# PSUM operands, another order of products and moved loads, with 512 moving columns in the gate and up projections

## What is computed

```python
# first network, per layer
y = hybrid_mixer(x, ...)            # chunked relative attention, latent attention, forgetting attention,
                                    # each with a gated projection, summed, times w_out
x = layer_norm(alpha * x + y, ...)
x = layer_norm(alpha * x + memory_cross_attention(x, mem, ...), ...)
x = layer_norm(alpha * x + swiglu_ffn(x, ...), ...)
# swiglu_ffn: gu = x @ w_gu; (silu(gu[..., :2816]) * gu[..., 2816:]) @ w_down

# second network, per layer: modulate(rmsnorm(x)), then a mixer of spatial gating (gelu, layernorm over a chunk),
# differential attention with a norm per head, and a short convolution; x += gate * (m @ wo); then
def conv_ffn(h, w_up, cw, cb, w_down):
    u = dwconv3(h @ w_up, cw) + cb           # three taps along the tokens
    g, val = jnp.split(u, 2, axis=-1)
    return (jax.nn.silu(g) * val) @ w_down
```

## Time and profile before

| what | value |
|---|---|
| median of three runs | 2719.44 us (2719.43 to 2723.04) |
| time of the profiled execution | 2722.86 us |
| its span | 2721.1 us |
| granted clock of TensorE, mean | 0.997 |
| TensorE matmul busy | 2677.6 us (98%), 21551 |
| VectorE busy | 1063.0 us (39%) |
| ScalarE busy | 1411.5 us (52%) |
| Gpsimd busy | 1953.0 us (72%) |
| DMA | 182 GB/s |

### The profile page before, as it was taken

One profiled execution on the slowest core, in us unless ns is written; L12 is line 12 of the kernel. 1 busy time (PEld: TensorE's weight loads), 2 busy tenths in 40 slices (PEclk: granted clock), 3 DMA queues, 4 the chain that ended last, 5 costly groups with the idle time before them and its releaser, 6 DMA issues.

```text
span 2721.1 us, 51137 instructions
## 1 busy us (share of the span) xinstructions
PE 2677.6 (98%) x21551; PEld 2505.1 (92%) x21551; DVE 1063.0 (39%) x2123; ACT 1411.5 (52%) x1936; POOL 1953.0 (72%) x816
## 2 busy tenths in 40 slices
PE   8999999999999999999999999999999999999999
PEld 8899989989899899989999998788999988989999
DVE  2433331134334422434434343545443345543434
ACT  5655554447565544455654446456544455565443
POOL 6657668856567488687687887766778877558787
PEclk9999999999999999999999999999999999999999
DMA  7555465565455655564454555544445565445453
GB/s 279 207 193 202 161 243 186 181 224 194 183 218 196 224 183 183 200 205 158 149 169 156 185 187 190 184 147 132 149 159 187 181 214 168 132 132 171 158 184 132
DMA packets 137093, 495.74 MB, mean 182 GB/s; under 512 B 15136, under 2 KB 17440, under 8 KB 135968
## 3 DMA queue, kind: packets, MB, share of 16 engines
q1 hardware_dynamic: 132480, 480.55, 52.4%
q10 hardware_dynamic: 4384, 11.93, 1.2%
HBM read 489.27 MB, written 3.15 MB: 181 GB/s over the span
## 4 chain that ended last, share of the span: by engine, by line
PE 94%; DVE 3%; ACT 2%; DVEq 1%; issue 0%; ACTq 0%; DMA 0%; SPq 0%
PE lin L578 19%; PE lin L582 18%; PE lin L579 18%; PE aux L578 5%; PE aux L579 5%; PE aux L582 5%; PE lin L618 4%; PE lin L619 4%; PE lin L622 4%; PE aux L1103 2%; PE aux L1121 1%; PE aux L799 1%; PE aux L767 1%; PE lin L767 1%; PE aux L1110 1%; DVE Z L1698 1%
## 5 line engine op out<-in xcount | busy, mean ns | idle before, releaser
L547 POOL TENSOR_TENSOR wlo<-raw,whi 128x1024 fp32r<-128x1024 f32 x812 | 1952.8, 2425 | 759.1 <-ACT whi L1210 758.5
L1210 ACT ACTIVATE whi<-raw 128x1024 fp32r<-128x1024 f32 x812 | 845.9, 1057 | 741.4 <-PE lin L582 518.6
L578 PE MATMUL lin<-in_hi,whi 128*128 128x256 f32 x3520 | 880.9, 287 | 20.4 <-ACT whi L1210 8.7
L579 PE MATMUL lin<-in_lo,whi 128*128 128x256 f32 x3520 | 867.2, 283 | 0.0
L578 PEld LDWEIGHTS lin<-in_hi,whi 128*128 128x128 f32 x3520 | 676.1, 192 | 55.9 <-issue 35.1
L579 PEld LDWEIGHTS lin<-in_lo,whi 128*128 128x128 f32 x3520 | 676.9, 192 | 0.5
L582 PE MATMUL lin<-in_hi,wlo 128*128 128x256 f32 x3520 | 501.8, 283 | 0.0
L582 PEld LDWEIGHTS lin<-in_hi,wlo 128*128 128x128 f32 x3520 | 458.4, 193 | 0.0
L578 PE MATMUL aux<-br_hi,whi 128*128 128x256 f32 x880 | 219.1, 283 | 0.0
L579 PE MATMUL aux<-br_lo,whi 128*128 128x256 f32 x880 | 218.9, 283 | 0.0
L578 PE MATMUL lin<-br_hi,whi 128*128 128x256 f32 x768 | 195.5, 288 | 0.0
(11 more groups left out here) (264 smaller groups left out, 3333.4 us busy)
## 6 DMA issues: line engine op xcount, KB each, us to landing
raw<-in_wstream SPq DMA_DIRECT2D x908, 512.0 KB, 3.4
Z<-in_rel ACTq DMA_DIRECT2D x2, 1536.0 KB, 9.5
Z<-in_mem_t ACTq DMA_DIRECT2D x2, 1024.0 KB, 5.3
kv_store<-Z ACTq DMA_DIRECT2D x2, 1024.0 KB, 8.6
Z<-kv_store ACTq DMA_DIRECT2D x2, 1024.0 KB, 11.4
x<-in_x_t SPq DMA_DIRECT2D x2, 512.0 KB, 6.0
Z<-in_ctx_t SPq DMA_DIRECT2D x1, 1024.0 KB, 5.0
out_x<-x SPq DMA_DIRECT2D x4, 256.0 KB, 2.2
```

Of the source, the lines that this page charges most:

```text
L547: pool.tensor_tensor(wlo[s][:, :], raw[i % RAWS][:, :], whi[s][:, :].bitcast(F32), ALU.subtract).then_inc(lo_pool, 1)
L578: pe.matmul(out, wh, xh, start=start, stop=False, skip_group_check=True)
L579: pe.matmul(out, wh, xl, start=False, stop=False, skip_group_check=True)
L1210: act.activation(whi[s % SLOTS][:, :], raw[i % RAWS][:, :], ACT.Copy).then_inc(hi_ready, 1)
```

## The change

In words:

- The high and low inputs become two halves of one tensor `in_both`. In the feed-forward blocks, hidden tiles 2 to 21 are made one at a time by `gate_up`: the high weight by high and low input as one matmul of 512 columns, into a whole PSUM bank, 256 columns of sums for each input; then the low weight by the high input, 256 columns, into the first half. VectorE adds the two halves with a `tensor_reduce` into SBUF. The convolution reads that sum and writes PSUM; the SiLU's input, the product and the rounding's input are in PSUM.
- A tile is two units. The order of units is: the first chunk, tile 2, then tile c and one down unit (three tiles behind) in turn. A half of `lin` is free only when the tile's low part is made.
- Where all eight input tiles are fresh, the first tile's products go in the order high weight by high input, low weight by high input, high weight by low input. The first two wait for `first_hi` alone, the last for `inputs_ready`.
- The merged halves, the GELU of v, and the root of the head norm (`head_root`, 16 columns of `aux`) stay in PSUM; the halves of `lin` are freed later for it.
- A preload of the Exp table is put behind the latent roots. The RMS norm of the last layer comes ahead of the DMA issues at the top of `second_layer`. The wait for the context's inverse goes behind the first hidden tiles.

The core of the diff:

```diff
 def ffn_units(chunk, unit, gu, down):
+    def gate_up(c):
+        at = c // 2 * CH + c % 2 * P
+        for k0 in (0, KD // 2):
+            unit(gu, [(k, at + up) for k in range(k0, k0 + KD // 2) for up in (0, 2 * P)], P)
+    chunk(gu, 0)
+    for c in range(2, HIDDEN):
+        gate_up(c)
+        if FIRST_DOWN <= c <= LAST_DOWN:
+            down_rows(c - FIRST_DOWN)
+    for c in range(LAST_DOWN - FIRST_DOWN + 1, HIDDEN - 2):
+        down_rows(c)
...
-        in_hi, in_lo = sb("in_hi", KD * T, F32R), sb("in_lo", KD * T, F32R)
+        in_both = ctx.enter_context(nc.sbuf_tensor("in_both", [P, 2, KD * T], F32R))
+        in_hi, in_lo = in_both[:, 0, :], in_both[:, 1, :]
...
@@ feature_units (token_units alike) @@
+                        if len(fresh) == KD and ks == (0,):
+                            pe.wait_ge(first_hi, t.next(first_hi))
+                            for j, (c, w) in enumerate(tiles):
+                                pe.matmul(lin[0:w, p, j * T:(j + 1) * T], wh[:, c:c + w], tile(xh, base), start=(j % 2 == 0), stop=False,
+                                          skip_group_check=True)
+                            low_part(low)
+                            for j, (c, w) in enumerate(tiles):
+                                low_product(lin[0:w, p, j * T:(j + 1) * T], wl[:, c:c + w], tile(xh, base), False)
+                            pe.wait_ge(inputs_ready, t.next(inputs_ready))
+                            for j, (c, w) in enumerate(tiles):
+                                low_product(lin[0:w, p, j * T:(j + 1) * T], wh[:, c:c + w], tile(xl, base), False)
+                            continue
...
@@ TensorE @@
+            def gate_up(p, after=()):
+                pe.wait_ge(lin_free[p], t.next(lin_free[p]))
+                for k0 in (0, KD // 2):
+                    wh, wl, low = next_unit()
+                    ...
+                    for k, up, w in blocks:
+                        pe.matmul(lin[:, p, up * CH:(up + 1) * CH], wh[:, w], in_both[:, :, k * T:(k + 1) * T],
+                                  start=(k == 0), stop=(k == KD - 1), skip_group_check=True)
+                    low_part(low)
+                    for k, up, w in blocks:
+                        mm = low_product(lin[:, p, up * CH:up * CH + T], wl[:, w], tile(in_hi, k), k == KD - 1)
...
@@ ScalarE, first_fill @@
+                act.preload_act_table(ACT.Exp)
...
@@ ScalarE, ffn @@
+                def hidden(c, units, behind=0):
+                    hi_parts(units)
+                    ...
+                    act.activation(silu_tile(conv, c), gate, ACT.Silu).then_inc(glu_ready, 1)
+                    hi_parts(behind)
+                    act.wait_ge(hid_f32, t.next(hid_f32))
+                    act.activation(hidden_tile(br_hi, c), gated_tile(p), ACT.Copy).then_inc(hid_hi, 1)
+                for c in range(2, HIDDEN - 1):
+                    hidden(c, 3 if c > FIRST_DOWN else 2)
...
@@ VectorE, ffn @@
+                def hidden(c, count):
+                    p = (c + 1) % 2
+                    both, h = gate_and_up(p), gated_tile(p)
+                    chunk_done(count)
+                    u = summed(conv, c)
+                    i = dve.tensor_reduce(three(u, 2), both.rearrange("p a (s t) -> p a t s", s=2), AX.X, ALU.add)
+                    if conv:
+                        settle()
+                        convolved([u[:, i * T:(i + 1) * T] for i in range(2)], [both[:, i, 0:T] for i in range(2)], taps(c))
+                        settle().then_inc(conv_out, 1)
+                        value = both[:, 1, 0:T]
+                    else:
+                        ...
+                    dve.wait_ge(glu_ready, t.next(glu_ready))
+                    tt_(h, silu_tile(conv, c), value, ALU.mult).then_inc(hid_f32, 1)
+                    settle()
+                    dve.wait_ge(hid_hi, t.next(hid_hi))
+                    tt_(hidden_tile(br_lo, c), h, hidden_tile(br_hi, c).bitcast(F32), ALU.subtract).then_inc(hid_lo, 1)
+                    settle().then_inc(lin_free[p], 1)
...
@@ VectorE, first_layer @@
-                    out = merged[:, half(d)]
+                    out = lin[:, 1 - d, :]
                     chunk_done(2)
-                    tt_(out, zt(GATES + 16 + 4 * d, 4), lin[:, 1 - d, :], ALU.mult).then_inc(lin_free[1 - d], 1)
+                    tt_(out, zt(GATES + 16 + 4 * d, 4), out, ALU.mult)
                     settle()
                     tt_(out, out, two[:, half(d)], ALU.add)
...
-                evacuate(1, 4, zt(GB + 4, 4), func=ACT.Gelu_apprx_tanh)
+                hi_parts(4)
+                units_done()
+                act.activation(lin[:, 1, :], lin[:, 1, :], ACT.Gelu_apprx_tanh)
...
-                    vt = zt(GB + 4 + 2 * tt, 2)
-                    last = dve.tensor_scalar(vt, vt, small[:, 40 + 2 * tt:41 + 2 * tt], small[:, 14 + tt:15 + tt],
+                    last = dve.tensor_scalar(zt(GB + 4 + 2 * tt, 2), lin[:, 1, tt * CH:(tt + 1) * CH], small[:, 40 + 2 * tt:41 + 2 * tt], small[:, 14 + tt:15 + tt],
                                              ALU.subtract, ALU.mult)
...
-                ss, var, ok, r = small[:, 208:224], small[:, 160:176], small[:, 192:208], small[:, 176:192]
+                ss, var, ok, r = small[:, 208:224], small[:, 160:176], small[:, 192:208], head_root
```

More of the change, by code:

```diff
@@ L630, in token_units @@
                     for i, ks in enumerate(runs):
+                        if len(fresh) == KD and ks == (0,):
+                            pe.wait_ge(first_hi, t.next(first_hi))
+                            halves = [(lin[:, p, tt * CH:(tt + 1) * CH], slice(tt * P, (tt + 1) * P)) for tt in range(2)]
+                            for out, s in halves:
+                                pe.matmul(out, xh[:, s], wh[:, 0:CH], start=True, stop=False, skip_group_check=True)
+                            low_part(low)
+                            for out, s in halves:
+                                token_low(out, xh[:, s], wl[:, 0:CH], False)
+                            pe.wait_ge(inputs_ready, t.next(inputs_ready))
+                            for out, s in halves:
+                                token_low(out, xl[:, s], wh[:, 0:CH], False)
+                            continue
                         for k in ks:
@@ L1467, in ffn, with first_tiles @@
             def ffn(conv, context_norm=False):
-                def hidden(j, units, behind=0):
-                    p, b = j % 2, j % 3
+                def first_tiles(units):
                     hi_parts(units)
@@ new lines, in ffn @@
+                first_tiles()
+                if context_norm:
+                    dve.wait_ge(inverse_wide, t.next(inverse_wide))
+                    copy(ctx_scale, inverse_out(0)).then_inc(ctx_inverse, 1)
+                    settle()
+                for c in range(2, HIDDEN):
+                    hidden(c, 3 if FIRST_DOWN < c < HIDDEN - 1 else 2)
+                    if context_norm and c % 4 == 1 and c < HIDDEN - 2:
+                        context_quarter(c // 4 - 1)
+                lo_parts(3)
```

213 lines of the change are left out of this document (107 added, 106 removed).

## The result

The changed kernel takes **2684.32 us** (median of 4 runs, 2683.75 to 2685.24), beside 2720.69 us (2719.43 to 2723.04) for the kernel before in the same comparison: ratio 0.9866, 95% interval 0.9849 to 0.9883. The prediction was 2681.7 us with a range from 2672 to 2704. The profiled execution took 2683.82 us; its span is 39.2 us shorter than that of the earlier trace rows, where the sum of the prediction had 37.7.

The account below looks back on a forecast made before the run. TensorE's matmuls were taken to bound the kernel; 21.3 - 2.0 + 8.4 + 2.8 + 2.0 + 3.3 + 1.9 + 0 = 37.7 us, against the median of 2719.44, gave 2681.7 us, range 2672 to 2704.

Parts of the forecast that it names:

- Bound by TensorE: Whole kernel: it ends when TensorE has got through its matmuls, which make up 94% of the chain that ended last.
- 512 columns, 21.3: Gate and up of five feed-forward blocks: 1600 pairs merged into 512-column matmuls, 13.3 ns less each, 21.3 us saved.
- a pair costs 0.2400 now and 0.2267 after: Gate and up: cost in us of two 256-column products against one of 512, taken from the nearest 512-column row.
- rival (1): Gate and up: a 512-column product over two runs costs what two of 256 do; gain 16.4, time 2703.0, chance 0.12.
- Block starts, -2.0: Starts of three convolution blocks: TensorE waits for VectorE to free halves of `lin`, 0.67 us a block, 2.0 us lost.
- 0.2 us before the third tile: Convolution block start: TensorE's wait for a half of `lin` after one tile, until VectorE's four-tile convolution ends.
- 0.45 before the fourth: Convolution block start: TensorE's next wait for its half of `lin`, since VectorE is done with the third tile at t + 14.5.
- the lower of my two bounds: VectorE's reduction adding a tile's two halves: 1.22 us by the nearest row, bounded by twice that, 2.4.
- PSUM operands, 13.2: Waits removed by reading from PSUM: spatial gating 8.4 us, merged halves of the mixer 2.8, head norm's scale 2.0.
- Product order, 3.3: Eight starts on fresh input: 0.5 us saved at five after an RMS norm, 0.25 at three after a layer norm.
- Moved loads, 1.9: Third RMS norm preceding a second-network layer: DMA issues no longer before ScalarE's squares, 1.9 us saved; bound 3 us of loss.
- Table load, 0: Preload of Exp: gains 0, as TensorE's 2.4 us wait behind the copy of the values stays; bound 2.4 saved.

Follow-up runs that it names:

- doubled and quadrupled reductions: The changed kernel with the reduction that adds a tile's two halves done twice, 2691.99 us, or four times, 2818.21 us.
- sixteen-and-sixteen kernel: The changed kernel with each tile's products ordered as sixteen high of 512 columns, then sixteen low of 256: 2688.71 us, ratio 0.9869.
- one-run kernel: The changed kernel with one contiguous run of 512 high-input columns as moving operand in gate and up, low-input products left out: 2684.59 us, ratio 0.9854.
- undone kernel: The changed kernel with the old order of products behind a fresh input: 2687.91 us, ratio 0.9863.
- the one with many pauses: The changed kernel with the reduction that adds a tile's two halves done four times: 2818.21 us, ratio 1.0349.

## Why the prediction was right, and where it wasn't

**Bound by TensorE: right.** Every term that shortened TensorE's own work or a wait of it came back as time, and 95 us more of VectorE cost only what lay at the block starts. The doubled and quadrupled reductions show the edge of this.

**512 columns, 21.3: mis-sized, 16.3.** The step that failed is "a pair costs 0.2400 now and 0.2267 after". The pitch of 0.2267 came from the earlier trace rows, a stage in which every product has 512 columns; in the new loop eight of 512 alternate with eight of 256, and each return to 512 costs 0.027 us, 200 times: 5.4 us, of which the narrow groups give back 1.4 while nine slow groups cost 1.0 more. The sixteen-and-sixteen kernel shows it as a price per passage, and the one-run kernel that the form of the operand has no part in it. What lies behind the 0.027 us is open; the trace places it in the first five wide products, and where narrow products follow wide ones it doesn't come. The Trainium skill (TensorE: Matmul & The Clock Gate, "Back-to-back issue gap") gives 2.5 ns beyond the columns as the gap of an isolated matmul, and the 4.0 us in rival (1) is an estimate from it; the trace has four times that.

**Block starts, -2.0: the sign right, the size half.** The 0.2 us before the third tile was not there (0.14 at most), and the 0.45 before the fourth came as 0.23, 0.24 and 0.58. The reduction took its 1.22 us, the lower of my two bounds.

**PSUM operands, 13.2: right against this kernel before, 14.5.** Undone in the changed kernel they cost 11.1. The difference lies in one place,'s 7.61 us: its first operation began 6.9 us before the end of a run of subtractions of Gpsimd. The Trainium skill says that a PSUM operand keeps fp32 at the lower rate (VectorE: DVE Perf Modes, "Why PSUM operands drop a tier"), and the trace agrees where Gpsimd is idle: 0.535 us from SBUF against 0.80 from PSUM for one normalisation. It decided nothing here, since Gpsimd is busy at these places: no SBUF pair took less than 3.55 us, the PSUM form took 1.53 (my sum had 1.4, from an operation of another kind).

**Product order, 3.3: 4.1.** I took half for the three starts after a layer norm, since VectorE's three operations a tile would take it back; they gave 0.5 too, and the undone kernel lost 3.6 by its median.

**Moved loads, 1.9: right**, 2.0 between before and after; undone in the changed kernel they cost 1.4 at the place and 1.5 by the medians, with a wait of 1.1 instead of 1.6. None of the 3 us of loss that I had as a bound came. **Table load, 0: right**, by the kernel without the preload.

**What the sum hadn't: the clock.** The profiled execution of before had two half-clock stretches more than that of after, 2.8 us in all. That was luck, and it made good over half of the 5.0 that the first term lacked; product order, block starts and PSUM operands each gave 0.8 to 1.3 us more than their terms. So the span of 2681.9 is nearer to the sum than its terms were. The median came out 2.6 us over the forecast. Half of this, 1.25, is the base: I put the 37.7 against the median of the runs shown, 2719.44; beside the changed kernel before's median was 2720.69, and 2724 in the later comparisons. The other 1.3 is the change itself, 36.4 us by the medians and 36.35 by the terms without the clock.

## What to carry to other kernels

A pitch read from a stage in which all products have one width is a lower bound for a loop that mixes widths: look for rows with the same alternation, or leave a margin per change of width (0.020 us for the way there and back here), and put products of one width together where no small product of another chain stands behind them. A VectorE operation between SBUF and SBUF beside a busy Gpsimd has no fixed duration (a pair that takes 1.53 us from PSUM took 3.6 to 7.6 here, though one of them took only 0.535 with Gpsimd idle): on the path, read its operand from PSUM, and price the move by the typical place and not by the worst. Before a difference of 2 us is explained, compare the granted clock of both traces window by window.

## What the hardware showed that was not expected

- A group of 512-column products behind 256-column ones takes 0.027 us more than its pitch, whether it has eight products or sixteen, all of it in the first five; the narrow group behind is 0.007 us shorter than its pitch.
- A moving operand of two runs of 256 columns streams as fast as one run of 512.
- TensorE's granted clock fell to 0.50 (1.2 GHz) for about 3.4 us, two to four times in an execution and nine times in the one with many pauses, at places that changed between executions of one kernel; with discarded products in one kind of pause there were three.
- At that clock products of 256 columns start 0.2133 us apart, at the full clock 0.1200: half the clock is not twice the time, and a stretch costs 1.2 to 1.6 us.
- A VectorE operation on 128x512 with its tensor inputs in SBUF took 0.535 us with Gpsimd idle and 1.0 to 7.1 us beside Gpsimd's subtractions; from PSUM it took 0.80 beside them.
- A reduction over 1024 elements of PSUM takes 1.22 us with 2 outputs and with 512.
